# A hybrid RWKV-7 and latent-attention layer on one core: latents split once into fp32r pairs, all heads' values computed ahead of the sweeps, two slabs parked in HBM

## Chip, core and metric

The program runs on one core of a Trainium2 chip, in one launch. The metric is the device time of that core in microseconds; lower is better. TensorE does the matmuls (PE in the rows, PEld for its weight loads), VectorE is DVE, ScalarE is ACT, GpSimd is POOL, and the loads are issued from SyncE (SP).

## What is computed

One decoder layer over 1024 tokens of width 1024, in float32. The part that matters here is the latent attention (MLA):

```python
h = x @ w_in                                   # 2464 columns: r, k, v, ..., c_q (384), c_kv (256), k_pe (32)
q  = (rms_norm(c_q)  @ w_uq ).reshape(S, 8, 64 + 32)     # 32 rotary columns per head
kv = (rms_norm(c_kv) @ w_ukv).reshape(S, 8, 64 + 64)     # k_nope, v
s  = where(causal, q @ k.T * scale, -inf)
y_mla = softmax(s) @ v                         # per head, 128-query blocks
```

An RWKV-7 group uses the columns r, k, v of the same `h`; then follow the output projection, two LayerNorms and a feed-forward with 4096 hidden columns.

## The kernel before, in words

`hT` holds the transposed projection as 20 slabs of 128 columns by 1024 tokens: r is slabs 0 to 3, k 4 to 7, v 8 to 11, the latents c_q 14 to 16 and c_kv 17 and 18, the rotary key 19.
`project_in` computes `hT` slab by slab, latents first; ACT scales a slab out of PSUM (L283), DVE blends in the token shift (`mix`, L333). The latents are normalised in place (L397). The last pair of slabs is 12 and 13.

`mla` is a software pipeline over 8 heads. PE's order is written out in `sweep`: for each block of 128 keys, `st` (scores by three products, L593), ACT's exponential (L680), `pv` (probabilities by values, float32, L608), and in between, by the table `TURNS`, the pieces of the next head, which share PSUM banks 0 and 1:

```python
TURNS = {0: ("q", None), 1: ("k", None), 2: ("v", 7), 3: (6, 5), 4: (4, 3), 5: (2, 1), 6: (0, "m")}
```

`q_item` (L521) is 6 float32 matmuls of 512 columns, `k_item` (L531) 4 with 64 output rows, `v_item` (L541) 16 with 64 columns; the numbers are score blocks whose row maxima DVE takes (L747), and "m" transposes the maxima. `take` waits on `a_free`: bank 0 or 1 is handed back by the engine that read it. DVE's order per head is: remainder of q (L722), the two rotary products (L734, L735, from a copy `q_pe` that ACT made, L663), first part of the reciprocal for the head before (L761), remainder of k (L722), second part of that reciprocal, the quotient (L767), then all the maxima. Heads 0 and 1 come without the reciprocal parts. Ahead of the heads DVE clears a tile, rounds the rotary key for both buffers and the mask constants (L708 to L717). The eight heads run in loops of two. SP loads a head's weights two heads ahead (L497) and clears two HBM scratch areas at the start (L505).

`rwkv_inputs` follows; its SP part begins at L933, its first masked product goes out at L944, and `rwkv_chunks` reads slabs r, k and v of `hT`.

Of the kernel before, what the change touches and what calls it, by code (L numbers as in the profile page):

```python
# [153 lines left out]
def project_in(nc, mem, k, x, w_in, positions):  # L154
# [12 lines left out]
    sums = ps[:, 4, 0:RT * TT * 2].rearrange("p (c t h) -> p c t h", c=RT, t=TT)  # L167
    first = T_CQ // 2
# [16 lines left out]
    with ExitStack() as ctx:  # L185
# [12 lines left out]
            nc, ctx, "a_keys_squared", "a_keys_summed", "a_keys_rooted", "a_rotated", "a_ones_in")  # L198
        block = ctx.enter_context(nc.Block())
# [3 lines left out]
        def _(sp):  # L203
# [18 lines left out]
            with sp.Fori(0, first) as i:  # L222
                load(i, i + early)

# [47 lines left out]
        def _(act):  # L272
# [44 lines left out]
            nc.scalar.activation(k.key_norm[:], sums, ACT.Sqrt).then_inc(keys_rooted, 1)  # L317
            pair(6, 6 + early)

        @block.vector  # L320
        def _(dve):
# [72 lines left out]
            def normalise(n):  # L394
                tile0, tiles, gain, _ = LATENTS[n]
                for c in range(tiles):
                    nc.vector.scalar_tensor_tensor(hT[:, tile0 + c, :], hT[:, tile0 + c, :],  # L397
                                                   cols[:, gain + c:gain + c + 1], root[n][:], ALU.mult, ALU.mult)
# [23 lines left out]
            step.mark(nc.vector.reciprocal(k.key_norm[:], k.key_norm[:]))  # L422
            for j in range(2):
                mix(j, first - 1, trips - 1)

def mla(nc, mem, k, t):
# [3 lines left out]
    trig = mem.at("trig", 118, [P, S])  # L431
    q_hi = [mem.at(f"q_hi{p}", 126 + 4 * p, [P, S], F32R) for p in range(2)]
    q_lo = [mem.at(f"q_lo{p}", 134 + 4 * p, [P, S], F32R) for p in range(2)]
    k_hi = [mem.at(f"k_hi{p}", 142 + 4 * p, [P, S], F32R) for p in range(2)]
    k_lo = [mem.at(f"k_lo{p}", 150 + 4 * p, [P, S], F32R) for p in range(2)]
    v_one = [mem.at(f"v_one{p}", 158 + 4 * p, [P, TT, P]) for p in range(2)]
    probs = [mem.at(f"probs{n}", 166 + 4 * n, [P, S]) for n in range(3)]
    w_uq = [mem.at(f"w_uq{p}", 178 + 1.5 * p, [P, QLT, P]) for p in range(2)]
    w_ukv = [mem.at(f"w_ukv{p}", 181 + p, [P, KVLT, P]) for p in range(2)]
    rot_a = mem.at("rot_a", 183, [P, S])  # L440
    rot_b = mem.at("rot_b", 187, [P, S])
    recip, y_full = k.att_recip, k.att_y
    att = k.att
    q_pe = mem.at("q_pe", 203, [P, S])
# [21 lines left out]
    TAKES = [("q", (0, 1)), ("k", (0, 1)), ("v", (0,))]  # L466
# [11 lines left out]
    with ExitStack() as ctx:  # L478
        in_sem, trig_ready, key_ready, causal_rr, ones_set = sems(
            nc, ctx, "b_in", "b_trig_ready", "b_key_ready", "b_causal_r", "b_ones_set")  # L480
        q_pe_done, zeroed, zeros_out = sems(nc, ctx, "b_q_pe_done", "b_zeroed", "b_zeros_out")
        w_in = sems(nc, ctx, "b_w_in0", "b_w_in1")
        q_hi_done, k_hi_done, rot_ready, q_ready, m_ready = sems(
# [11 lines left out]
        @block.sync  # L495
        def _(sp):

            def load(h, p):
                sp.dma_start(w_uq[p][:], t["w_uq"][h]).then_inc(w_in[p], 16)
                sp.dma_start(w_ukv[p][:], t["w_ukv"][h]).then_inc(w_in[p], 16)  # L500
# [7 lines left out]
            with sp.Fori(1, NH // 2) as i:  # L508
                for p in range(2):
                    sp.wait_ge(item[0], USES[0] * (2 * i + p - 2) + nth("v", 0) + 1)  # L510
                    load(2 * i + p, p)

        @block.tensor
        def _(pe):
# [6 lines left out]
            def q_item(h, p, i, first):  # L521
                pe.wait_ge(w_in[p], 32 * (i + 1))
                for b in range(2):
                    if not first:
                        take(h, "q", b)
                    for c in range(QLT):
                        last = nc.tensor.matmul(ps[:, b, :], w_uq[p][:, c, :],
                                                hT[:, T_CQ + c, b * HALF:(b + 1) * HALF],
                                                start=c == 0, stop=c == QLT - 1)
                    last.then_inc(item[b], 1)  # L530

            def k_item(h, p):
                pe.wait_ge(q_pe_done, h + 1)
                for b in range(2):
                    take(h, "k", b)
                    for c in range(KVLT):
                        last = nc.tensor.matmul(ps[lo64, b, :], w_ukv[p][:, c, 0:HD],
                                                hT[:, T_CKV + c, b * HALF:(b + 1) * HALF],
                                                start=c == 0, stop=c == KVLT - 1)
                    last.then_inc(item[b], 1)  # L540

            def v_item(h, p):
                take(h, "v", 0)
                for tt in range(TT):
                    for c in range(KVLT):
                        last = nc.tensor.matmul(ps[:, 0, tt * HD:(tt + 1) * HD],
                                                hT[:, T_CKV + c, tt * P:(tt + 1) * P], w_ukv[p][:, c, HD:2 * HD],
                                                start=c == 0, stop=c == KVLT - 1)
                last.then_inc(item[0], 1)
# [48 lines left out]

            def pv(h, p, kt):
# [4 lines left out]
                for b in range(2):  # L604
# [3 lines left out]
                    last = nc.tensor.matmul(ps[:, O[b], lo - b * HALF:HALF], v_one[p][:, kt, :],  # L608
# [4 lines left out]
            def sweep(h, p, i, more):  # L613

                def turn(what):
# [3 lines left out]
                    if what == "q":  # L619
                        q_item(nh, np_, i + p, False)  # L620
                    elif what == "k":
                        k_item(nh, np_)
                    elif what == "v":
                        v_item(nh, np_)
# [13 lines left out]
            q_item(0, 0, 0, True)  # L638
            k_item(0, 0)
            v_item(0, 0)  # L640
# [6 lines left out]
            with pe.Fori(0, NH // 2 - 1) as i:  # L647
                for p in range(2):
                    sweep(2 * i + p, p, i, True)
            sweep(NH - 2, 0, NH // 2 - 1, True)  # L650
            sweep(NH - 1, 1, NH // 2 - 1, False)

        @block.scalar
        def _(act):
            def front(h, p, n):

                if n == 0:
# [3 lines left out]
                    if not (type(h) is int and h == 0):  # L661
                        act.wait_ge(q_ready, h)
                    nc.scalar.activation(q_pe[hi64, :], flat(A, hi64), ACT.Copy).then_inc(q_pe_done, 1)  # L663
                if n == 1:
                    for b in range(2):
                        act.wait_ge(item[b], USES[b] * h + nth("k", b) + 1)
                    nc.scalar.activation(k_hi[p][lo64, :], flat(A, lo64), ACT.Copy).then_inc(k_hi_done, 1)
                if n == 2:
                    act.wait_ge(item[0], USES[0] * h + nth("v", 0) + 1)
                    nc.scalar.activation(v_one[p][:, :, 0:HD], ps[:, 0, :].rearrange("p (t d) -> p t d", d=HD),  # L670
                                         ACT.Copy).then_inc(a_free[0], 1)
# [4 lines left out]
            def sweep(h, p, more):  # L676
                for kt in range(TT):
# [8 lines left out]
                    if more and kt == 2:  # L686
                        front(h + 1, 1 - p, 2)
# [7 lines left out]
            for n in range(4):  # L695
                front(0, 0, n)
            with act.Fori(0, NH // 2 - 1) as i:
                for p in range(2):
                    sweep(2 * i + p, p, True)
            sweep(NH - 2, 0, True)  # L700
            sweep(NH - 1, 1, False)

        @block.vector
        def _(dve):
            step = k.dve_steps.on(dve)
            V = nc.vector

            V.memset(zeros, 0.0).then_inc(zeroed, 1)  # L708
# [10 lines left out]
            def low_part(lo, hi):  # L719
# [1370 lines left out]
```

## Time and profile before

| | us |
|---|---|
| median of the runs (1686.79 to 1690.92) | 1690.69 |
| the profiled execution's own time | 1691.39 |
| its span, first to last instruction | 1689.6 |
| projection (start to the last slab's blend) | 0 to 265.5 |
| attention (`mla`) | 265.7 to 554.3 |
| feed-forward and last norm | from about 760 |

The span is 1.8 us less than the execution's time. Over the whole span PE is busy 92 percent, DVE 53, ACT 18, POOL 12, and TensorE's mean granted clock is 0.956 of full speed. A busy share says which engine has the most to do, not which wait ends last; for that the timeline of one head is read. A timeline row is start, duration, engine, line, operation and how many were merged; a bracket gives the idle time before it and what ended that.

### The profile page before, as it was taken

To read this page: it belongs to the slowest core of one execution; us is meant where nothing else is said; L and a number is where in the kernel's file an instruction comes from. 1 tells how busy PE (TensorE), PEld (TensorE's weight loads), DVE (VectorE), ACT (ScalarE), POOL (GpSimd) and SP (SyncE) were. 2 spreads that over 40 slices of the span, in tenths; PEclk is the share of its full clock that TensorE was granted. 3 is DMA by queue.
4 is the path that set the end of the run, shared out by engine and by line. 5 is a ranking of instruction groups with operands and counts; after the bars stand their busy time and mean duration, and the time that the engine had idled before them with its cause. 6 is when DMAs were issued, how large, how long until landed. Compare 5 with 4: busy or idle time off the path is not lost. (4 is left out here: it accounts for less than half of the span.)

```text
span 1689.6 us, 26357 instructions
## 1 busy us (share of the span) xinstructions
PE 1546.1 (92%) x11192; PEld 1239.7 (73%) x11192; DVE 888.6 (53%) x1077; ACT 307.7 (18%) x431; POOL 209.0 (12%) x134
## 2 busy tenths in 40 slices
PE   6999997999999718999789799999999999999994
PEld 5887884656666418998578688888888888888873
DVE  3254444356656863334747645555555555555559
ACT  2112201233333602322200210000000000000001
POOL 0000003124323350000106100000000000000005
PEclk8999988899999869999989899999999999999997
DMA  4111103000000162121050111111111111111002
GB/s 166 50 50 42 45 13 126 9 8 8 16 0 1 31 87 60 42 49 53 12 199 0 61 65 50 50 50 50 50 50 50 50 50 50 50 50 50 25 1 99
DMA packets 80507, 82.91 MB, mean 49 GB/s; under 512 B 63136, under 2 KB 65696, under 8 KB 78384
## 3 DMA queue, kind: packets, MB, share of 16 engines
q1 hardware_dynamic: 72176, 81.28, 14.6%
q10 hardware_dynamic: 8256, 0.52, 0.5%
q8 instruction: 61, 1.00, 0.2%
q14 instruction: 14, 0.11, 0.0%
HBM read 70.18 MB, written 11.60 MB: 48 GB/s over the span
## 5 line engine op out<-in xcount | busy, mean ns | idle before, releaser
L1907 DVE TENSOR_TENSOR x<-banks,x 128x512 f32<-128x512 f32 x256 | 171.4, 688 | 99.1 <-PE banks L1835 99.0
L1835 PE MATMUL banks<-w_hi,hid_hi 128*128 128x512 f32 x480 | 187.4, 390 | 2.3 <-DVE x L1907 2.3
L1835 PE MATMUL banks<-w_hi,hid_lo 128*128 128x512 f32 x480 | 187.4, 391 | 0.0
L1835 PE MATMUL banks<-w_lo,hid_hi 128*128 128x512 f32 x480 | 187.4, 390 | 0.0
L122 PE MATMUL banks<-x1T_hi,w_hi 128*128 128x512 f32 x512 | 157.7, 389 | 2.3 <-DVEq L1928 2.3
L122 PE MATMUL banks<-x1T_lo,w_hi 128*128 128x512 f32 x512 | 157.6, 389 | 0.0
L122 PE MATMUL banks<-x1T_hi,w_lo 128*128 128x512 f32 x512 | 157.6, 389 | 0.0
L1892 DVE TENSOR_TENSOR squared<-relu 128x1024 f32<-128x1024 f32 x32 | 39.2, 1226 | 224.9 <-ACT relu L1856 224.9
L1856 ACT ACTIVATE relu<-banks 128x1024 f32<-128x1024 f32 x32 | 32.9, 1029 | 589.0 <-PE banks L122 589.0
L122 PEld LDWEIGHTS banks<-x1T_hi,w_hi 128*128 128x128 f32 x512 | 96.0, 188 | 22.4 <-DVEq L1928 2.5
L122 PEld LDWEIGHTS banks<-x1T_hi,w_lo 128*128 128x128 f32 x512 | 96.1, 188 | 20.0
L122 PEld LDWEIGHTS banks<-x1T_lo,w_hi 128*128 128x128 f32 x512 | 96.1, 188 | 20.0
L1835 PEld LDWEIGHTS banks<-w_hi,hid_hi 128*128 128x128 f32 x480 | 90.5, 189 | 21.5 <-DVE x L1907 2.7
L122 PE MATMUL banks<-xT_hi,win_hi 128*128 128x512 f32 x320 | 101.0, 397 | 4.8 <-DVE xT_lo L404 4.8
L1835 PEld LDWEIGHTS banks<-w_hi,hid_lo 128*128 128x128 f32 x480 | 90.5, 188 | 18.8
L1835 PEld LDWEIGHTS banks<-w_lo,hid_hi 128*128 128x128 f32 x480 | 90.4, 188 | 18.8
L1974 POOL TENSOR_TENSOR x<-x,ln_gain 128x1024 f32<-128x1024 f32 x5 | 11.8, 2370 | 718.2 <-ACT x L1868 718.2
L122 PE MATMUL banks<-xT_lo,win_hi 128*128 128x512 f32 x320 | 100.2, 395 | 0.0
L122 PE MATMUL banks<-xT_hi,win_lo 128*128 128x512 f32 x320 | 99.7, 393 | 0.0
L333 DVE SCALAR_TENSOR_TENSOR hT<-banks,cols,hT 128x1023 f32 (+1 forms) x20 | 25.7, 1283 | 138.4 <-ACT hT L283 138.3
L608 PE MATMUL banks<-probs,v_one 128*128 128x512 f32 (+3 forms) x192 | 75.5, 507 | 0.0
L131 DVE TENSOR_TENSOR w_lo<-w_raw,w_hi 128x1024 fp32r<-128x1024 f32 (+1 forms) x47 | 73.6, 1566 | 1.6
(270 smaller groups left out, 2773.4 us busy)
## 6 DMA issues: line engine op xcount, KB each, us to landing
w_raw<-in_w_ffn SPq DMA_DIRECT2D x32, 512.0 KB, 5.9
w_raw<-in_w_ffn SPq DMA_DIRECT2D x16, 1024.0 KB, 4.8
win_raw<-in_w_in SPq DMA_DIRECT2D x20, 512.0 KB, 3.5
x_tok<-in_x SPq DMA_DIRECT2D x8, 512.0 KB, 7.6
wout_raw<-in_w_out SPq DMA_DIRECT2D x8, 512.0 KB, 4.7
x<-in_x SPq DMA_DIRECT2D x1, 4096.0 KB, 18.1
layer_out<-x SPq DMA_DIRECT2D x8, 512.0 KB, 2.6
inv_d<-ym_lo SPq DMA_DIRECT2D x4, 512.0 KB
```

The lines of the kernel that those rows point to most:

```text
L122: last = nc.tensor.matmul(out, w[:, kt, :], r(kt, b), start=kt == 0 and n == 0, stop=kt == tiles - 1 and n == 2)
L131: nc.vector.tensor_tensor(lo, raw, hi.bitcast(F32), ALU.subtract).then_inc(lo_sem, 1)
L333: nc.vector.scalar_tensor_tensor(hT[:, 2 * i + j, 1:S], flat[:, 0:S - 1], cols[:, bass.ds(C_MU + 2 * i + j, 1)], hT[:, 2 * i + j, 1:S], AL ...
L608: last = nc.tensor.matmul(ps[:, O[b], lo - b * HALF:HALF], v_one[p][:, kt, :], probs[kt % 3][:, lo:(b + 1) * HALF], start=kt == 0, stop=kt ...
L1835: last = nc.tensor.matmul(ps[:, 4 + n % 4, :], a[q][:, j, tok], w[:, j, col], start=j == 0 and m == 0, stop=j == GRP - 1 and m == 2)
L1856: A(relu[j][:], flat(2 * j), ACT.Relu).then_inc(relu_done, 1)
L1892: V.tensor_tensor(squared[j][:], relu[j][:], relu[j][:], ALU.mult).then_inc(relu_free, 1)
L1907: return V.tensor_tensor(piece, ps[:, 4 + n % 4, :], piece, ALU.add).then_inc(added, 1)
L1974: step.mark(G.tensor_tensor(acc[:, tt, :], acc[:, tt, :], gain[:], ALU.mult))
```

## The change

Five things. (1) After normalisation each of the five latent slabs is split once into `lat_hi` (ACT) and `lat_lo` (DVE). The room comes from slabs r, which SP stores to HBM (`r_d`) before; v is stored too (`v_d`), since attention's tiles now lie there. `rwkv_inputs` loads both back ahead of its other constants. (2) `q_item` becomes 18 fp32r matmuls, for which DVE splits each head's `w_uq`. (3) All heads' values are computed once, after head 0's keys, by 48 fp32r matmuls of 512 columns (`value_items`); `v_item` is gone. (4) `k_item` stays float32, but its two 512-token halves go to output rows 0 to 63 and 64 to 127. (5) ACT's copy `q_pe` is gone: DVE takes the rotary products straight from PSUM, and now before the remainder of q. The loops over heads are written out.

```diff
@@ project_in
+            for j in range(2):
+                sp.wait_ge(h_mixed[j], early + 2)
+            sp.dma_start(k.r_d, hT[:, T_R:T_R + RT, :]).then_inc(r_out, 16)
...
+            sp.dma_start(k.v_d, hT[:, T_V:T_V + RT, :]).then_inc(v_out, 16)
+            sp.wait_ge(v_out, 16)
...
+            act.wait_ge(r_out, 16)
+            for c in range(QLT + KVLT):
+                act.wait_ge(normed, c + 1)
+                nc.scalar.activation(k.lat_hi[c][:], hT[:, T_CQ + c, :], ACT.Copy).then_inc(latents_hi, 1)
             pair(6, 6 + early)
...
+            for c in range(QLT + KVLT):
+                dve.wait_ge(latents_hi, c + 1)
+                nc.vector.tensor_tensor(k.lat_lo[c][:], hT[:, T_CQ + c, :], k.lat_hi[c][:].bitcast(F32), ALU.subtract)
             for j in range(2):
                 mix(j, first - 1, trips - 1)
@@ mla
-    TURNS = {0: ("q", None), 1: ("k", None), 2: ("v", 7), 3: (6, 5), 4: (4, 3), 5: (2, 1), 6: (0, "m")}
+    TURNS = {0: ("q", None), 1: ("k", None), 2: (None, 7), 3: (6, 5), 4: (4, 3), 5: (2, 1), 6: (0, "m")}
...
-            load(0, 0)
+            load(0)
+            for h in range(NH):
+                sp.dma_start(wv_raw[:, :, h, :], t["w_ukv"][h][:, :, HD:2 * HD]).then_inc(wv_in, 16)
             sp.dma_start(causal[:], t["causal"]).then_inc(in_sem, 16)
-            load(1, 1)
+            load(1)
...
+                pe.wait_ge(w_split[p], h // 2 + 1)
                 for b in range(2):
                     if not first:
                         take(h, "q", b)
+                for c in range(QLT):
+                    for n, (w, r) in enumerate(((wq_hi, lat_hi), (wq_hi, lat_lo), (wq_lo, lat_hi))):
+                        for b in range(2):
+                            last = nc.tensor.matmul(ps[:, b, :], w[p][:, c, :], r[c][:, b * HALF:(b + 1) * HALF],
+                                                    start=c == 0 and n == 0, stop=c == QLT - 1 and n == 2)
...
             def k_item(h, p):
-                pe.wait_ge(q_pe_done, h + 1)
                 for b in range(2):
                     take(h, "k", b)
+                for c in range(KVLT):
+                    for b in range(2):
+                        last = nc.tensor.matmul(ps[64 * b:64 * b + 64, b, :], w_uk[p][:, c, :],
                                                 hT[:, T_CKV + c, b * HALF:(b + 1) * HALF],
...
-            q_item(0, 0, 0, True)
+            q_item(0, 0, True)
             k_item(0, 0)
-            v_item(0, 0)
+            value_items()
...
         @block.vector
+            split_w(0)
+            dve.wait_ge(wv_in, 16 * NH)
+            split2(nc, dve, wv_raw[:], wv_hi[:], wv_lo[:], wv_rounded, 1, wv_split)
+            split_w(1)
             V.memset(zeros, 0.0).then_inc(zeroed, 1)
...
             def front_q(h, p, first=False):
-                dve.wait_ge(q_hi_done, h + 1)
-                low_part(q_lo[p], q_hi[p])
-                dve.wait_ge(q_pe_done, h + 1)
+                for b in range(2):
+                    dve.wait_ge(item[b], USES[b] * h + nth("q", b) + 1)
...
+                V.tensor_tensor(rot_a[pe32, :], flat(A, pe32), trig[pe32, :], ALU.mult).then_inc(rot_ready, 1)
+                V.tensor_tensor(rot_b[pe32, :], flat(A, sw32), trig[sw32, :], ALU.mult).then_inc(rot_ready, 1)
+                dve.wait_ge(q_hi_done, h + 1)
+                low_part(q_lo[p], q_hi[p], False)
...
+            for h in range(2, NH):
+                front_q(h, h % 2)
+                invert(h - 2, 0)
+                front_k(h, h % 2)
+                invert(h - 2, 1)
+                leave(h - 2, h % 2)
+                maxima(h, h % 2)
+                if h + 2 < NH:
+                    split_w(h + 2)
@@ rwkv_inputs
             sp.dma_start(w_lora[:], t["w_lora"]).then_inc(loaded, 16)
+            sp.dma_start(hT[:, T_V:T_V + RT, :], k.v_d).then_inc(reloaded, 16)
+            sp.dma_start(hT[:, T_R:T_R + RT, :], k.r_d).then_inc(reloaded, 16)
             sp.dma_start(k.gate[:], t["gate_g2"]).then_inc(later_in, 16)
...
+            sp.wait_ge(reloaded, 32)
```

## Rows read from the trace of the kernel before

**Rows 1.** The page: busy time, share of the span and instructions of each engine

```profile
PE 1546.1 (92%) x11192; PEld 1239.7 (73%) x11192; DVE 888.6 (53%) x1077; ACT 307.7 (18%) x431; POOL 209.0 (12%) x134
```

**Rows 2.** Timeline, one steady head (front of head 5 within the sweep of head 4)

```profile
444.73 1.02 ACT L660 ACTIVATE q_hi<-banks 64x1024 fp32r<-64x1024 f32 x1 [3.77 <-PE banks L527]
...
445.78 1.28 DVE L722 TENSOR_TENSOR q_lo<-banks,q_hi 64x512 fp32r<-64x512 f32 x2 [8.81 <-ACT q_hi L660]
...
446.92 3.64 PE L537 MATMUL banks<-hT,w_ukv 128*64 128x512 f32 x8 [0.89 <-ACT q_pe L663]
447.10 1.22 DVE L734 TENSOR_TENSOR rot_a<-q_pe,trig 32x1024 f32<-32x1024 f32 x1
...
450.60 1.02 ACT L667 ACTIVATE k_hi<-banks 64x1024 fp32r<-64x1024 f32 x1 [2.87 <-PE banks L537]
...
452.96 4.95 DVE L761 RECIPROCAL att_recip<-att 64x768 f32<-64x768 f32 x1
...
453.50 3.68 PE L546 MATMUL banks<-w_ukv,hT 128*128 128x64 f32 x32
...
459.19 1.29 DVE L747 TENSOR_REDUCE row_max_parts<-banks 128x1 f32<-128x512 f32 x2
...
460.30 0.68 PE L561 MATMUL banks<-k_hi,q_hi 96*128 96x512 f32 x2
```

**Rows 3.** Timeline of PE, eleven fp32r matmuls of 512 columns apart: first and last

```profile
1499.62 0.39 PE L1835 MATMUL banks<-w_lo,hid_hi 128*128 128x512 f32 x1
...
1501.89 0.39 PE L1835 MATMUL banks<-w_hi,hid_lo 128*128 128x512 f32 x1
```

**Rows 4.** Timeline of PE in the RWKV chunks, products on both halves of the array

```profile
661.17 0.57 PE L1298 MATMUL banks<-inverse_t,product 64*64 64x64 f32 x14
```

**Rows 5.** Timeline, DVE's first maxima of head 1, which have no reciprocal before them

```profile
325.20 1.29 DVE L747 TENSOR_REDUCE row_max_parts<-banks 128x1 f32<-128x512 f32 x2 [6.06 <-PE banks L561]
```

**Rows 6.** Timeline, DVE's remainder of q for heads 3 and 4

```profile
378.98 1.28 DVE L722 TENSOR_TENSOR q_lo<-banks,q_hi 64x512 fp32r<-64x512 f32 x2 [8.83 <-ACT q_hi L660]
...
412.10 1.28 DVE L722 TENSOR_TENSOR q_lo<-banks,q_hi 64x512 fp32r<-64x512 f32 x2 [8.34 <-ACT q_hi L660]
```

**Rows 7.** Timeline of the start of attention

```profile
265.73 0.34 SPq L499 DMA_DIRECT2D w_uq<-in_w_uq  x1
...
266.97 2.91 DVE L710 CAST k_hi<-key_rot 32x1024 fp32r<-32x1024 f32 x2
...
272.66 0.07 DVE L770 MEMSET row_max_parts<- 128x16 f32 x1
...
278.30 3.65 PE L537 MATMUL banks<-hT,w_ukv 128*64 128x512 f32 x8 [2.22 <-ACT q_pe L663]
...
289.24 1.19 PE L561 MATMUL banks<-k_hi,q_hi 96*128 96x512 f32 x2 [0.78 <-ACT v_one L670]
```

**Rows 8.** DMA issues of the chunk stage, 256-byte pieces: size, median us to landing

```profile
inverse_t<-inv_t_d SPq DMA_DIRECT2D x18, 64.0 KB, 2.4
```

**Rows 9.** Timeline, SP's issues of such copies

```profile
635.80 1.26 SPq L1202 DMA_DIRECT2D inverse_t<-inv_t_d  x2
```

**Rows 10.** Groups by line and shape, DVE's remainder of a 128x1024 weight tile

```profile
L131 DVE TENSOR_TENSOR win_lo<-win_raw,win_hi 128x1024 fp32r<-128x1024 f32 x20 | 24.5, 1226 | 0.7
```

**Rows 11.** Timeline of PE in `rwkv_inputs`, after a wait

```profile
596.41 3.07 PE L979 MATMUL banks<-kk,beta 64*64 64x64 f32 x64 [2.62 <-DVE kk L1065]
```

**Rows 12.** Windows: length, busy time of PE, PEld, DVE, ACT, POOL, granted clock, DMA

```profile
597.00:598.00 1.00, 1.00 (x30) 1.00 (x27) 1.00 (x2) 0.00 (x0) 1.00 (x1) 0.59 0.14 31
598.00:602.00 4.00, 3.79 (x92) 3.60 (x89) 2.77 (x2) 0.00 (x0) 0.58 (x1) 0.67 0.73 141
```

**Rows 13.** Timeline of the end of the projection: the last slab's blend

```profile
264.18 1.28 DVE L333 SCALAR_TENSOR_TENSOR hT<-banks,cols,hT 128x1023 f32<-128x1023 f32 x1 [9.59 <-ACT hT L283]
```

**Rows 14.** The page: a load of 4 MB, size and us to landing

```profile
x<-in_x SPq DMA_DIRECT2D x1, 4096.0 KB, 18.1
```

**Rows 15.** Timeline of SP in `rwkv_inputs`: the first store that waits for the constants

```profile
592.82 5.99 SPq L944 DMA_DIRECT2D low_d<-low_keys  x4
```

More of the change, by code:

```diff
@@ L221, in _ @@
                 load(i, i - first)
-            with sp.Fori(0, first) as i:
+            with sp.Fori(0, 4) as i:
                 load(i, i + early)
+            for j in range(2):
+                sp.wait_ge(h_mixed[j], early + 2)
+            sp.dma_start(k.r_d, hT[:, T_R:T_R + RT, :]).then_inc(r_out, 16)
+            with sp.Fori(4, first) as i:
+                load(i, i + early)
+            for j in range(2):
+                sp.wait_ge(h_mixed[j], early + 6)
+            sp.dma_start(k.v_d, hT[:, T_V:T_V + RT, :]).then_inc(v_out, 16)
+            sp.wait_ge(v_out, 16)
         @block.tensor
@@ L507, in _ @@
                 sp.dma_start(part, zeros[0:part.shape[0], :]).then_inc(zeros_out, 16)
[L508 to L511, printed above, removed]
+            for h in range(2, NH):
+                sp.wait_ge(w_split[h % 2], h // 2)
+                for b in range(2):
+                    sp.wait_ge(item[b], USES[b] * (h - 2) + nth("k", b) + 1)
+                load(h)
         @block.tensor
@@ L525, in q_item @@
                         take(h, "q", b)
[L526 to L530, printed above, removed]
+                for c in range(QLT):
[3 more added lines that the diff above has]
+                                                    start=c == 0 and n == 0, stop=c == QLT - 1 and n == 2)
+                            if c == QLT - 1 and n == 2:
+                                last.then_inc(item[b], 1)
@@ L545, in v_item @@
                     for c in range(KVLT):
[L546 to L549, printed above, removed]
+                        for n, (r, w) in enumerate(((lat_hi, wv_hi), (lat_lo, wv_hi), (lat_hi, wv_lo))):
+                            last = nc.tensor.matmul(ps[:, 2 + tt % 6, :], r[QLT + c][:, at],
+                                                    w[:, c, :, :].rearrange("p h d -> p (h d)"),
+                                                    start=c == 0 and n == 0, stop=c == KVLT - 1 and n == 2)
@@ L597, in st, with values_and_ones @@
                 last.then_inc(st_ready, 1)
+            def values_and_ones(h, kt):
+                pair = v_all[:, kt, h // 2, :, :].rearrange("p a d -> p (a d)")
+                return pair[:, 64 * (h % 2):64 * (h % 2) + P]
             def pv(h, p, kt):
@@ L611, in pv, with sweep @@
                 last.then_inc(pv_done, 1)
-            def sweep(h, p, i, more):
+            def sweep(h, p, more):
                 def turn(what):
@@ L646, in _ @@
             pe.wait_ge(ones_set, 1)
[L647 to L651, printed above, removed]
+            pe.wait_ge(v_out, TT)
+            for h in range(NH):
+                sweep(h, h % 2, h < NH - 1)
         @block.scalar
@@ L666, in front @@
                         act.wait_ge(item[b], USES[b] * h + nth("k", b) + 1)
[L667 to L671, printed above, removed]
+                    for b in range(2):
+                        nc.scalar.activation(k_hi[p][lo64, b * HALF:(b + 1) * HALF], ps[64 * b:64 * b + 64, b, :],
+                                             ACT.Copy).then_inc(k_hi_done, 1)
                 if n == 3:
@@ L694, in _ @@
             act.sem_inc(exp_done, T_FREE)
[L695 to L701, printed above, removed]
+            front(0, 0, 0)
+            front(0, 0, 1)
+            for tt in range(TT):
+                act.wait_ge(v_mm, tt + 1)
+                nc.scalar.activation(v_all[:, tt, :, 0:3:2, :],
+                                     ps[:, 2 + tt % 6, :].rearrange("p (i a d) -> p i a d", a=2, d=HD), ACT.Copy)\
+                    .then_inc(v_out, 1)
+            front(0, 0, 3)
+            for h in range(NH):
+                sweep(h, h % 2, h < NH - 1)
         @block.vector
@@ L823, in _ @@
             step.wait()
-            for p in range(2):
-                last = G.memset(v_one[p][:, :, HD:P], 1.0)
-            last.then_inc(ones_set, 1)
+            G.memset(v_all[:, :, :, 1, :].rearrange("p t i d -> p (t i) d"), 1.0).then_inc(ones_set, 1)
             pool.wait_ge(ones_set, 1)
```

125 lines of the change are left out of this document (66 added, 59 removed).

## The prediction

> **What bounds the kernel now.** I read the page first: PE is busy 92 percent [rows 1], and the change takes PE work away, which looks like a gain of the same size. A busy share is no critical path, so the timeline of one steady head comes next [rows 2]. There two things run side by side between the end of the q item (call it Q, 444.73, where ACT begins to read it) and the first maxima. PE runs scores, keys, values and `pv` with one gap of 0.89 us. DVE runs a fixed chain: remainder of q (1.28), two rotary products (1.22 each), reciprocal parts, remainder of k, 4.95 of reciprocal, quotient, and the first maximum begins at 459.19, Q+14.5. PE's next score block (qt 6) needs the bank that this maximum frees; it starts at 460.30, Q+15.6. Both arrive together: PE has no slack there and DVE has none either. The values item, which ends just before, is what keeps PE occupied while DVE inverts.
>
> **The change, part by part.** All sums stand against the profiled execution, 1691.4 us, which is 0.7 above the median of the runs (1690.7).
>
> *Queries.* Before, 12 instructions of 512 columns. Their pace is that of the keys, 8 in 3.64 with a tail of some 0.2 [rows 2], 0.427 us each: 5.1 us. After, 18 fp32r instructions at (1501.89 − 1499.62) / 10 = 0.227 us [rows 3]: 4.1 us. Gain 1.0 us per head, seven heads beside a sweep; it lies ahead of Q, on the path.
>
> *Values.* Before, 3.68 less the tail of some 0.2, 3.5 us per head, up to 457.0 [rows 2]. Gone.
>
> *Keys.* Before 8 × 0.427 = 3.4 us. The new order is half 0 (two passes), half 1 (two passes), twice over. Fourteen passes of 64 columns on distinct rows and columns of the array took 0.57 us [rows 4], where in turn, at 0.427 × 64 / 512 = 0.053 each, they would need 0.75: neighbours on separate array parts overlap. If halves that share all rows do so too, a pass of one half lies beside a pass of the other, and 8 passes take 5 slots, 2.1 us. Bounds: 1.7 (all in pairs) and 3.4 (none). I take 2.1.
> The Trainium skill (TensorEngine Tiling, Key Properties) says that tiles operate independently, and its list of configurations has 128×64 as two tiles; by that the item would take 1.7 to 2.1, and by a plain reading of in-order issue 3.4. No row of before has two halves over the same rows.
>
> *The chain after Q.* This part decides. DVE now does the rotary products first: 2.5 us, then the remainder of q, 1.3, and only that frees the banks. Keys start at Q+3.9; PE has finished its scores at 446.92 − 0.89, Q+1.3, so its gap grows from 0.9 to 2.6 us. Keys end at Q+6.2 (Q+5.8 before). ACT copies the halves in two pieces, between 0.5 (half of its 1.02) and 1.0 each; I take 0.6. Then remainder of k 1.3, reciprocal 4.95, quotient with its hand-over 1.25 (459.19 − 457.91): the first maximum begins at Q+15.1, against Q+14.5. PE: keys issued by Q+6.0, `pv` and scores 3.2 (450.33 to 453.50), no values, then 3.3 (457.02 to 460.30) brings it to block 6 at Q+12.5. The block waits for the first maximum, until Q+15.8, and its second half for the second, so what follows is 0.5 us later after Q than before. So the 3.5 us of values and 1.3 of keys turn into an idle of 3.3 us, and a steady head gains 1.0 − 0.5 = 0.5 us. Six heads (2 to 7): −3 us.
>
> *Head 1* has no reciprocal before its maxima; there DVE sat idle 6.06 us for PE [rows 5]. It gains in full: 1.0 + 3.5 + 1.3, less 1.7 of the longer gap: −4 us.
>
> *Written-out loops.* Remainder of q comes 33.1 us after its predecessor where a loop body runs on (378.98 to 412.10 [rows 6]) and 33.7 where the loop turns (to 445.78 [rows 2]). Three turns: between 0 and −2; I take −2. Fetching the longer program is between 0 and a few us; straight code elsewhere keeps PE busy, so 0.
>
> *Head 0.* PE cannot start the keys until the remainder of q has freed the banks, and DVE's queue has new work in front of it. SP starts at 265.7 [rows 7]; ten issues stand up to the last values load, nine of them 256-byte pieces at 0.63 [rows 9], and such a copy lands in 2.4 [rows 8]: about 274.2. Splitting the values' weights costs 1.2 [rows 10] plus a cast of less than that, a head's weights 0.8 more: 277. Then the old chain of clearing and casting, 266.0 to 272.7 [rows 7], so it ends near 283.7. Products and remainder: 287.5. Keys start there, not at 278.3 [rows 7], at half clock after so long a wait (5 × 0.85 = 4.3): 291.8. Then 48 fp32r matmuls, 10.9 us and about 1 for the clock's return: 303.8. The first score block follows; it was at 289.24 [rows 7]. +14 us, between +10 (loads land early, keys in pairs) and +17 (loads at half that pace). On the queue behind SP's new loads stand the mask, head 1's weights and the HBM clears; the mask is needed at 283, the clears at the end.
>
> *Clock.* A wait of 2.22 us at the start of attention left the keys at full pace (3.65 for 8 [rows 7], as in the steady head). A wait of 2.62 us [rows 11] was followed by a fall from 2.4 to 1.2 GHz 1.2 us later (granted clock 0.59 in that us [rows 12]). The new idle of 3.3 us before block 6 is past both, so I count one fall per head, 2 to 7. That fall was over after 3.4 us (0.59 of full speed in one us and 0.67 in the next four are 0.8 and 2.6 us at half [rows 12]). It costs half its length where PE is the busy one, which it is after block 6: 1.7 each, 6 of them, +10. The other gap, 2.6 us, lies at the edge; I count it at nothing and keep it as a rival.
> The Trainium skill (TensorE: Matmul & The Clock Gate, "A second HAM failure mode") says that TensorE's small idles between groups of matmuls can swing the clock; no number of mine is taken from it.
>
> *Projection.* ACT's 5 copies and DVE's 5 remainders (1.2 each) fall before the last slab, while PE works: DVE waited 9.59 us for the last blend [rows 13]. If they were late, the blend would be, by at most 5 × 1.2. The stores, 2 MB each, are half of a load of 18.1 us [rows 14], and v goes out with a whole slab pair of PE work to come. Zero.
>
> *Reload.* 4 MB ahead of the constants, 18 us on the queue [rows 14], so they land near 577 plus what attention loses; the first product that needs them goes out at 592.8 [rows 15]. Zero, and if that cover failed a few us.
>
> Sum: 1691.4 + 14 − 4 − 3 − 2 + 10 = 1706.4; against the median 1706.
>
> **Rivals.**
> *The clock holds.* The short idles let it stay up: 1696. For it: the 2.22 us wait. Against it: that waits of 2.62 us already told.
> *The wait before the keys.* Rotary products ahead of the remainder make 2.6 us of idle, equal to the one that told. If the clock falls there too, the keys run at half pace on DVE's chain: 1.9 us in each of 7 heads, +13: 1719. From 2.2 to 2.6 us it decides.
> *The halves do not overlap.* The change then does not do what it says: 1.3 us more per head on the chain, for 7 heads and head 0, +10: 1716.
> *PE work counts in full (faster).* If DVE's chain reached its maxima before PE does, at Q+12.5 or earlier, 2.6 us sooner than I add up, then all removed work would tell: queries 8, values 3.5 × 8 − 11 = 17, keys 10, loops 2, less head 0's late start of about 14 and the added gaps, which overlap in part: 1670. For it: PE's 92 percent. Against it: every term of that chain is a measured row, and the reciprocal stays.
>
> **How the numbers follow.** Forecast (1701 to 1711) 0.40. Clock holds 0.20; half of that falls within 0.3 percent, which is 5 us and about what a measurement of this kernel can tell from no change. Wait before the keys 0.13, no overlap 0.10, PE in full 0.17. So faster 0.17, same 0.10, slower 0.73. The range 1688 to 1720 leaves out most of the last case and the worst of the slower ones, some 2 in 10.
>
> **What would show it.** Right: first scores of head 1 some 14 us later; DVE's values split ahead of its clearing; PE waiting about 2.6 us before keys and 3.3 us before block 6 for a maximum; half clock after it; keys in 2.1 to 2.4 us; head 1's maxima no longer waiting for PE. Wrong: a head period well below 32 us, maxima that wait for PE, or the keys of head 0 starting before 285.

## The result, and the profile after

| | before | after |
|---|---|---|
| median of the runs, us | 1689.59 (1686.79 to 1690.92, 4 runs) | 1706.38 (1700.32 to 1709.89, 4 runs) |
| ratio, 95 percent interval | | 1.0098 (1.0063 to 1.0133) |
| the profiled execution's own time, and its span | 1691.39, 1689.6 | 1704.15, 1702.3 |
| mean granted clock | 0.956 | 0.943 |
| start of attention (first weight load) to the first score block of head 0 | 23.5 | 35.3 |
| attention, start to the load of `w_lora` | 289.1 | 306.4 |
| from there to the end | 1134.8 | 1131.2 |

The changed kernel was run a second time in a later batch: 1704.38, ratio 1.0097 (1.007 to 1.0124), as expected (1700 to 1710). It is slower: 16.8 us by the medians of each of the two batches (1706.38 against 1689.59, 1704.38 against 1687.61), 12.7 us between the two profiled executions. (Time and profile before gave 1690.69 as the median; that is the higher of the two middle values.) Medians here leave out four executions in a much slower state: two of the kernel before, 2022 and 2024 us, and two of experiment 2, 3151 and 3982 us.

All of the loss arises in attention. The other stages scatter by a few us from one execution to the next: the last row of the table was 1131.2 in this execution, 1134.5 in the second one, and 1134 to 1138 in all other kernels of this study, and attention began anywhere between 261.1 and 266.6 us. From here on the length of attention in the profiled execution is therefore read beside the time.

The page first: busy time by engine. Before it was 1546.1 for PE [rows 1].

```profile
PE 1521.8 (89%) x11032; PEld 1230.5 (72%) x11032; DVE 903.9 (53%) x1100; ACT 303.3 (18%) x434; POOL 208.6 (12%) x133
```

PE has 24 us less work, and the span is 12.7 us longer: the time in which PE does nothing grew by 37 us. Where it grew, the timeline of one steady head of the changed kernel says (front of head 6, within the sweep of head 5). It answers to [rows 2]; Q is 491.31, where DVE begins the rotary products.

```profile
491.31 1.22 DVE L782 TENSOR_TENSOR rot_a<-banks,trig 32x1024 f32<-32x1024 f32 x1 [5.29 <-PE banks L563]
...
493.83 1.28 DVE L771 TENSOR_TENSOR q_lo<-banks,q_hi 64x512 fp32r<-64x512 f32 x2
...
495.14 1.75 DVE L812 RECIPROCAL att_recip<-att 64x256 f32<-64x256 f32 x1
...
495.26 1.94 PE L574 MATMUL banks<-hT,w_uk 128*64 128x512 f32 x8 [2.71 <-DVE q_lo L771]
...
497.30 1.21 ACT L708 ACTIVATE k_hi<-banks 64x512 fp32r<-64x512 f32 x2 [3.79 <-PE banks L574]
...
498.54 1.41 DVE L771 TENSOR_TENSOR k_lo<-banks,k_hi 64x512 fp32r<-64x512 f32 x2 [1.65 <-ACT k_hi L708]
...
499.98 4.95 DVE L812 RECIPROCAL att_recip<-att 64x768 f32<-64x768 f32 x1
...
506.21 2.73 DVE L797 TENSOR_REDUCE row_max_parts<-banks 128x1 f32<-128x512 f32 x4
...
506.96 1.29 PE L603 MATMUL banks<-k_hi,q_hi 96*128 96x512 f32 x2 [3.44 <-DVE row_max_parts L797]
```

The keys wait 2.71 us for the remainder of q. The product of block 6 waits 3.44 us for the first maximum, which stands behind 4.95 of reciprocal on DVE. DVE in turn waits 5.29 us for the q item: within one head each engine waits for the other in turn. The wait before the keys comes back in heads 1 to 7, the one before block 6 in heads 2 to 7 (waits of the changed kernel from 300 to 554 us; a row is who waited for whom, total us, times, longest; the 11 of the first row include short ones):

```profile
PE banks L603 <- DVE row_max_parts L797: 21.2, 11, 3.5
PE banks L574 <- DVE q_lo L771: 18.9, 7, 2.7
```

What the clock does behind the wait before block 6 stands in the windows (length, busy time of PE, PEld, DVE, ACT, POOL, granted clock, DMA share, GB/s); the last row is another head's keys, those at 425.46, after the same wait of 2.70 us:

```profile
506.00:507.00 1.00, 0.04 (x1) 0.05 (x1) 0.97 (x3) 0.00 (x0) 0.74 (x1) 1.00 0.00 0
507.00:508.00 1.00, 0.97 (x2) 0.59 (x3) 0.93 (x2) 0.00 (x0) 1.00 (x1) 0.62 0.00 0
508.00:510.00 2.00, 2.00 (x6) 1.30 (x6) 0.81 (x2) 0.00 (x0) 1.92 (x2) 0.50 0.00 0
510.00:511.00 1.00, 1.00 (x4) 0.51 (x3) 0.00 (x0) 0.00 (x0) 0.56 (x1) 0.67 0.00 0
511.00:515.00 4.00, 4.00 (x23) 3.19 (x22) 2.60 (x5) 0.80 (x2) 0.00 (x0) 1.00 0.00 0
...
427.00:429.00 2.00, 2.00 (x7) 0.33 (x3) 0.10 (x1) 0.00 (x0) 1.92 (x2) 0.57 0.00 0
```

Half clock follows the wait before block 6 in each of the six heads that have it, for some 3.4 us in five of them and 6.8 us in head 3. The keys ran at full clock in heads 5 to 7 (1.94 us for 8), as in the head shown; in heads 1 to 4 they ran mostly at half (3.2 to 3.7 us; 3.54 at 425.46). The starts of the rotary products are 35.4, 36.9 and 35.7 us apart from head 2 to head 5, and 34.1 and 34.1 from there; before, a head took 33.1 to 34.0. Before, the granted clock was 1.00 over all of 310 to 554 us.

Head 0, on the timeline, answers to [rows 7]:

```profile
276.24 0.91 DVE L756 MEMSET ym_lo<- 128x1024 f32 x1 [0.16 <-issue]
...
281.63 1.22 DVE L782 TENSOR_TENSOR rot_a<-banks,trig 32x1024 f32<-32x1024 f32 x1 [0.36 <-DVE row_max_parts L822]
...
285.57 3.52 PE L574 MATMUL banks<-hT,w_uk 128*64 128x512 f32 x8 [9.06 <-DVE q_lo L771]
...
289.02 0.50 PE L588 MATMUL banks<-wv_hi,latent_hi 128*128 128x512 f32 x1
...
300.03 0.63 PE L603 MATMUL banks<-k_hi,q_hi 96*128 96x512 f32 x2
```

DVE's old clearing chain starts only at 276.24, behind the split of the values' weights; PE waits 9.06 us for it, and the first score block stands at 300.03.

### The profile page after: what moved, and what is told of

Its sections match the earlier page's. It is cut to its first block and busy times, and to the rows that moved or that the text cites. A ratio compares the mean times of both kernels' runs of the same rounds, so it can differ in the third digit from the quotient of the medians.

```text
span 1702.3 us, 25673 instructions
## 1 busy us (share of the span) xinstructions
PE 1521.8 (89%) x11032; PEld 1230.5 (72%) x11032; DVE 903.9 (53%) x1100; ACT 303.3 (18%) x434; POOL 208.6 (12%) x133
## 3 DMA queue, kind: packets, MB, share of 16 engines
q1 hardware_dynamic: 75952, 89.67, 15.8%
## 5 line engine op out<-in xcount | busy, mean ns | idle before, releaser
L2025 POOL TENSOR_TENSOR x<-x,ln_gain 128x1024 f32<-128x1024 f32 x5 | 11.8, 2369 | 716.9 <-ACT x L1919 716.9
L655 PE MATMUL banks<-probs,v_all 128*128 128x512 f32 (+3 forms) x192 | 84.1, 556 | 0.0
```

Source lines behind the costliest of these rows:

```text
L655: last = nc.tensor.matmul(ps[:, O[b], lo - b * HALF:HALF], values_and_ones(h, kt), probs[kt % 3][:, lo:(b + 1) * HALF], start=kt == 0, sto ...
L2025: step.mark(G.tensor_tensor(acc[:, tt, :], acc[:, tt, :], gain[:], ALU.mult))
```

## The experiments

All compare with the changed kernel's 1704.4 to 1706.4 us and its 306 us of attention.

**1. Half of the reciprocal ahead of the query item.** DVE sits idle 5.29 us before the rotary products; this puts work there.

```diff
-                cut = (slice(0, S // 4), slice(S // 4, S))[n]
+                cut = (slice(0, S // 2), slice(S // 2, 3 * S // 4), slice(3 * S // 4, S))[n]
...
             for h in range(2, NH):
-                front_q(h, h % 2)
                 invert(h - 2, 0)
-                front_k(h, h % 2)
+                front_q(h, h % 2)
                 invert(h - 2, 1)
+                front_k(h, h % 2)
+                invert(h - 2, 2)
                 leave(h - 2, h % 2)
```

> Edit to the changed kernel: the reciprocal for the head before is cut in three and its first half (512 columns, about 3.3 us) is done before the rotary products, where DVE sits idle 5.3 us; the rest stays in its two old places. Chain theory (DVE's fixed chain after Q sets when block 6 may start, and the idle there drops the clock): the wait before block 6 shrinks from 3.4 us to at most 0.5, the fall of the clock after it goes, a steady head takes about 29.5 us instead of 34.1, six heads give 28 us: about 1678 us where the changed kernel has 1706. Rival (the heads are bound by what PE and the clock do, and the place of the reciprocal is indifferent): within 3 us of 1706.

Measured: 1681.02, ratio to before 0.9958 (0.9938 to 0.9979), attention 278.2. The same waits:

```profile
PE banks L574 <- DVE q_lo L771: 18.9, 7, 2.7
...
PE banks L603 <- DVE row_max_parts L797: 2.5, 7, 0.5
```

Of the two waits only the one before block 6 went, from 3.5 to at most 0.5 us, and heads take 29.4 to 30.6 us. That one wait with the half clock behind it is 23 to 25 us of time. The removed PE work was real; it stood behind DVE's queue. The wait before the keys is as long as ever, and in six of the seven heads the keys behind it ran partly at half clock (2.7 to 3.6 us, 1.94 in the seventh). So this clock loss is still in the 1681; experiments 3 and 9 take it away.

**2. The same in the kernel before**, where by [rows 2] DVE and PE reach the maxima together.

> Edit to the kernel before: the same move of the reciprocal's first half ahead of the front of q. Theory (before the change PE's values item filled the time of DVE's chain, so both arrived together and PE had no gap): at most 1 us per head, 1684 to 1690 us. Rival (DVE's chain bound the kernel before, too): 3 us per head, about 1672 us.

Measured: 1688.91 against 1689.55 of the kernel before in the same batch, ratio 0.999 (0.9976 to 1.0004). The reorder is worth nothing that can be told from no change where PE has the values to compute meanwhile (heads 2 to 7 are 33.0 to 33.5 us apart, before 33.1 to 34.0). So the gain of experiment 1 is the change's own, held back by DVE, and not one that either kernel could have had.

**3. The idle filled.** Matmuls whose results nobody reads, in both gaps (9 before the keys of heads 1 to 7, 13 before block 6 of heads 2 to 7): the waits shrink to 0.65 and 0.5 us, DVE's chain stays.

```diff
                     if what == "k":
+                        fill(h, 0, 9)
+                    if what == 6 and nh >= 2:
+                        fill(h, 2, 13)
```

> Edit to the changed kernel: in the two gaps of a head PE runs idle-time matmuls of 512 fp32r columns into a score bank that is free (9 before the keys, 13 before block 6), so PE is busy but nothing is done sooner; the output is untouched. Clock theory (each wait costs its own length and, on top, half speed for 3.4 us after it): granted clock 2.4 GHz throughout the sweeps, block 6 no earlier after Q, but a head about 1.7 us shorter, six heads, and as much again for three of the waits before the keys: 1691 to 1696 us. Rival (the falls cost nothing since DVE is late anyway): 1706.

Measured: 1689.9, ratio 1.0003 (0.9983 to 1.0022), attention 289.8. Windows, in which only PE's work and the clock matter:

```profile
314.00:430.00 116.00, 110.92 (x509) 77.82 (x507) 73.33 (x92) 32.30 (x46) 40.84 (x18) 1.00 0.04 10
430.00:540.00 110.00, 105.31 (x496) 74.87 (x495) 70.90 (x85) 32.03 (x47) 33.83 (x15) 1.00 0.01 3
```

In the changed kernel the same view has 0.87 for 314 to 430 and 0.94 for 430 to 554. More work for PE, and 15 to 16 us less time. Block 6 still starts at Q+15.6 (457.42 against 441.78 in head 5), so the gaps are as long as before, and what has changed is the clock behind them: this is the half clock's price alone. Heads 2 to 7 take 32.6 us each. It is not the whole loss of the change, since the gaps themselves stay behind the filling; experiment 1 removes one of them and gets 9 us more.

**4. Both key halves on output rows 0 to 63**, one after the other, so that they cannot lie beside each other.

```diff
-                for c in range(KVLT):
-                    for b in range(2):
-                        last = nc.tensor.matmul(ps[64 * b:64 * b + 64, b, :], w_uk[p][:, c, :],
+                for b in range(2):
+                    for c in range(KVLT):
+                        last = nc.tensor.matmul(ps[lo64, b, :], w_uk[p][:, c, :],
```

> Edit to the changed kernel: both 512-token halves of the keys go to output rows 0 to 63, one half after the other, as before the change. Theory (the pairing halves the item, and the item lies on DVE's chain): the keys take 3.6 us instead of 1.9 and the first maximum comes 1.5 us later in each head, seven heads and head 0: about 1718 us. Rival (the keys hide beside something): 1706.

Measured: 1725.19, ratio 1.0222 (1.0194 to 1.0249), attention 325.5, a steady head 37.5 us. Timeline:

```profile
466.34 5.03 PE L574 MATMUL banks<-hT,w_uk 128*64 128x512 f32 x8 [2.71 <-DVE q_lo L771]
...
480.86 1.29 PE L603 MATMUL banks<-k_hi,q_hi 96*128 96x512 f32 x2 [3.18 <-DVE row_max_parts L797]
```

and the window behind that block:

```profile
480.00:486.00 6.00, 5.14 (x11) 3.43 (x12) 3.14 (x7) 0.00 (x0) 4.23 (x2) 0.50 0.00 0
```

Worse than expected by 7 us. The halves side by side save not 1.3 us per head but 1.7 at full clock and more behind a wait: here the item ran partly at half clock in every head (5.0 to 5.3 where full clock gave 3.64 in [rows 2]). The half clock behind block 6 also lasts 6.8 us in each of the six heads, twice as long as in most heads of the changed kernel. The pairing, with what it spares in clock, is worth 19 to 21 us to the changed kernel.

**5. Head 0's queries ahead of its values** on DVE.

```diff
-            split_w(0)
-            dve.wait_ge(wv_in, 16 * NH)
-            split2(nc, dve, wv_raw[:], wv_hi[:], wv_lo[:], wv_rounded, 1, wv_split)
-            split_w(1)
             V.memset(zeros, 0.0).then_inc(zeroed, 1)
+            split_w(0)
...
+            dve.wait_ge(wv_in, 16 * NH)
+            split2(nc, dve, wv_raw[:], wv_hi[:], wv_lo[:], wv_rounded, 1, wv_split)
```

> Edit to the changed kernel, DVE's order at the start of attention alone: clearing and rotary-key rounding first, then head 0's query weights, then the values' weights; the weights of head 1 are split after the remainder of head 0's keys. Theory (the keys of head 0 waited for DVE's queue, 9.1 us of PE idle): keys of head 0 start at about 280.5 instead of 285.6, the first score block at about 293.5 instead of 300.0, the sweeps are unchanged: 6.5 us less than the changed kernel, about 1700. Rival (the start is bound by the loads or by the clock): within 2 us of 1706.

Measured: 1701.03, ratio 1.0069 (1.0042 to 1.0096); the first score block at +30.9 after the start of attention against +35.3, so 4.4 us earlier, of the 6.5 expected. Of the 2.1 that are missing, 0.7 lie before the keys, since PE begins its q item 1.1 us later and ends it 0.6 later. The other 1.4 lie behind them: keys and values take 14.5 us as in the changed kernel, partly at half clock, where the expectation left 13.0. Attention is 299.7 us, 6.7 less than the changed kernel's; the further 2.3 us arise in the sweeps, where the keys ran slow in three heads, not four. The keys of head 0 (timeline):

```profile
282.64 2.82 PE L574 MATMUL banks<-hT,w_uk 128*64 128x512 f32 x8 [4.04 <-DVE q_lo L770]
```

**6. The copy of the rotary parts put back** (heads 1 to 7): ACT copies them, DVE takes the remainder of q first, banks come free earlier.

```diff
+                        nc.scalar.activation(q_pe[hi64, :], flat(A, hi64), ACT.Copy).then_inc(q_pe_done, 1)
...
+                if h:
+                    dve.wait_ge(q_hi_done, h + 1)
+                    low_part(q_lo[p], q_hi[p], False)
+                    dve.wait_ge(q_pe_done, h)
...
+                    V.tensor_tensor(rot_a[pe32, :], q_pe[pe32, :], trig[pe32, :], ALU.mult).then_inc(rot_ready, 1)
+                    V.tensor_tensor(rot_b[pe32, :], q_pe[sw32, :], trig[sw32, :], ALU.mult).then_inc(rot_ready, 1)
```

> Edit to the changed kernel: ACT's copy of the rotary half of q is back for heads 1 to 7 (in the room of a latent tile that only the values read), and DVE takes the remainder of q first and the rotary products after it, from the copy. Theory: keys start about Q+2.2 instead of Q+3.95, PE's wait before them is 0.9 instead of 2.7 us and no fall of the clock follows it; but the products then stand between the remainder of q and the remainder of k, so the first maximum comes only about 0.6 us earlier, and the wait before block 6 stays at 3.5 to 4 us. 0.6 in seven heads and 2 us in each of the three heads that fell there: 1696 to 1700 us. Rival (the keys' early start carries through to the end of the head): 1.7 us per head, 1694 or less with no fall: about 1690.

Measured: 1703.33, ratio 1.0084 (1.0057 to 1.0112), level with the changed kernel's 1704.38 of the same batch: a miss by the time. Attention is 299.6 us against 306.0, a gain of the size expected, but it began 4.8 us later (266.6 against 261.8) than in the changed kernel's execution of that batch; with a scatter of that size outside attention, four executions can't tell the two apart. The mechanism was missed in any case. The keys waited 1.25 us in place of 2.7 and ran in 1.94 in all seven heads; and then (waits, and a window behind block 7 of head 5, which starts at 464.68):

```profile
PE banks L606 <- POOL q_lo L869: 21.2, 7, 3.0
```

```profile
466.00:472.00 6.00, 5.77 (x13) 3.34 (x13) 3.36 (x5) 0.70 (x1) 4.23 (x2) 0.50 0.00 0
```

Block 7 needs GpSimd's rotated queries, which come 7.1 us after the second product (three operations of 2.34). Put behind the remainder and a copy, they end last. Half clock follows that wait of 3.0 us in six of the seven heads, each time for 6.8 us. So the change's order, products first, pays 1.5 us before the keys to be on time there: GpSimd's last operation ends at 500.97 and block 7 starts at 501.22 in the changed kernel.

**7. Experiments 1, 5 and 6 together.**

> The changed kernel with the early reciprocal, the order of head 0 and the rotary copy together. Theory: the reciprocal no longer hides behind the keys, so the keys' earlier start now carries through: a steady head takes about 28 us (29.4 with the early reciprocal alone), the start is 6.5 us shorter: about 1664 us, under both kernels. Rival (the parts share one gain): about 1675.

Measured: 1694.45, ratio 1.0032 (1.0014 to 1.0051), attention 292.0. A miss by 20 to 30 us: the wait for GpSimd is 3.0 us in each of 7 heads again, with half clock behind it in six. The rotary copy alone is what parts this version from experiment 8, and it costs 19 us there.

**8. Experiments 1 and 5 alone.**

> The changed kernel with the two edits that helped alone: half of the earlier head's reciprocal ahead of the query item, and head 0's queries ahead of its values. Theory (the two act in different places, one in heads 2 to 7 and one in head 0, so they add): 1681 less the 4 us that head 0's order gave by itself, about 1677, with the wait of the block-6 product at 0.5 us and block 7 of head 0 at +31. Rival: the half clock of head 0 takes it back, 1681.

Measured: 1675.1 (1669.9 to 1679.31), ratio 0.9925 (0.9898 to 0.9953), attention 274.3, the wait before block 6 at most 0.3 us. They add: 4 us of attention less than experiment 1, and 1677 was expected.

**9. Keys one turn later,** behind the first product with the earlier head's values, and the reciprocal in two halves, both ahead of the key remainder. The cut is against experiment 8; the third call of `invert` goes too.

```diff
-    TURNS = {0: ("q", None), 1: ("k", None), 2: (None, 7), 3: (6, 5), 4: (4, 3), 5: (2, 1), 6: (0, "m")}
+    TURNS = {0: ("q", None), 1: (None, "k"), 2: (None, 7), 3: (6, 5), 4: (4, 3), 5: (2, 1), 6: (0, "m")}
...
-                cut = (slice(0, S // 2), slice(S // 2, 3 * S // 4), slice(3 * S // 4, S))[n]
+                cut = (slice(0, S // 2), slice(S // 2, S))[n]
```

> As the kernel with both edits, with the rest of the reciprocal between the query item and the key halves; the key turn stands one place later in TensorE's order, behind the first product with the values of the earlier head (1.7 us). Theory (what costs is a TensorE wait of over 2 us with half clock behind it): the product fills most of the 2.7 us wait ahead of the keys, which falls to about 1.0, the heads take 28.5 to 29.5 us, and the time is 1665 to 1671. Rival (the keys come later by what the product takes, and so do key halves, maxima and block 6): the wait ahead of block 6 comes back at 2 us or more, 1677 to 1685. A third: GpSimd's rotation of the queries ends last, as in the kernel that copied the rotary parts back, and TensorE waits for it ahead of block 7, 1680 to 1695.

Measured: 1665.31 (1659.42 to 1667.74), ratio 0.9854 (0.9832 to 0.9876), attention 262.6, a steady head 28.5 us. Its waits, and then a head on its timeline:

```profile
PE banks L574 <- DVE q_lo L770: 6.9, 7, 1.0
PE banks L603 <- POOL q_lo L856: 6.8, 7, 1.0
```

```profile
429.70 1.88 PE L655 MATMUL banks<-probs,v_all 128*128 128x512 f32 x4
432.57 1.94 PE L574 MATMUL banks<-hT,w_uk 128*64 128x512 f32 x8 [0.99 <-DVE q_lo L770]
...
438.32 0.74 PE L603 MATMUL banks<-k_hi,q_hi 96*128 96x512 f32 x2 [0.95 <-POOL q_lo L856]
```

Both waits are 1.0 us, the keys took 1.94 us in all seven heads, the granted clock was 1.00 from 314 to 430, and GpSimd is the next in line. One head took 30.1 us: between 466 and 476 the clock fell once all the same, although no wait there was longer than 1.0 us. The two edits, PE's turn and the place of the reciprocal, were not run apart. This version beats the kernel before by 1.5 percent and the changed one by 40 us.

**10. The query item in float32 again,** 12 instructions on the upper part of the latents with the raw weights; the remainders of latents and weights in the query are left out.

```diff
-                    for n, (w, r) in enumerate(((wq_hi, lat_hi), (wq_hi, lat_lo), (wq_lo, lat_hi))):
+                    for b in range(2):
+                        last = nc.tensor.matmul(ps[:, b, :], w_uq[p][:, c, :],
+                                                lat_hi[c][:, b * HALF:(b + 1) * HALF].bitcast(F32),
```

> The changed kernel with the query projection as float32 on the latents' upper part alone, 12 instructions, in place of 18 fp32r ones (the raw weights, no remainders of weight or latents in the query: that part of the computation is left out). By the measured pace of float32 keys, 0.427 us each, the item takes 5.1 us in place of 18 by 0.227, 4.1 us. Theory (the query item lies on the path that starts each head in the changed kernel, since block 6 waits for a chain that begins at its end): 1.0 us for each of 8 heads, 8 us above the changed kernel, about 1713. Rival (VectorE's chain from the earlier head ends last, so the item's own length is hidden): within 3 us of the changed kernel.

Measured: 1711.59, ratio 1.0134 (1.0115 to 1.0154), 5 to 7 us above the changed kernel, attention 313.3, 7 us longer. On the timeline the item takes

```profile
491.16 5.31 PE L562 MATMUL banks<-latent_hi,w_uq 128*128 128x512 f32 x12
```

So three fp32r products in place of float32 are worth the 1 us per head that the sum gave them, and this saving reaches the end: it lies ahead of Q.

## Why the prediction was right

The stretches of the profiled executions, forecast and measured, against before:

| stretch | forecast | measured |
|---|---|---|
| projection, up to the first weight load | 0 | −1.0 |
| from there to the first score block of head 0 | +14 | +11.8 |
| from there to the end of the q item of head 2 (head 1) | −4 | −5.6 |
| heads 2 to 7, loops, clock (−3 − 2 + 10) | +5 | +11.1 |
| after attention | 0 | −3.6 |
| sum | +15 | +12.7 |

*The chain after Q* was the step that decided, and it held: first maximum at Q+14.9 (forecast 15.1, though its own terms add up to 14.9), block 6 at Q+15.65 (15.8), its wait 3.44 (3.3), the wait before the keys 2.7 (2.6). What it makes of a head without the clock shows in experiment 3: 32.6 us, where the loop bodies that ran on took 33.1, which is the 0.5 us of gain forecast. The rival in which PE's work counts in full needed a shorter chain; experiment 1 shows that it is DVE's order which kept it from coming true: 1681, and with head 0's order, PE's turn and the reciprocal moved too (experiment 9), 1665.

*Values.* Their 3.5 us per head turned into idle, as forecast, and experiment 2 shows it from the other side: with the values still in the sweep an early reciprocal is worth nothing that the runs can tell.

*Queries.* 1.0 us per head: the item took 4.1 us (486.96 to 491.06), and experiment 10 confirms that the difference reaches the end.

*Keys.* I took 2.1 us between 1.7 and 3.4. All in pairs was right: 1.94 with its tail, and 3.5 at half clock at the start. The Trainium skill (TensorEngine Tiling, Key Properties) says that tiles operate independently; the trace agrees, with 8 passes of 512 columns in 1.94 us against 3.64 [rows 2], although neighbours in the order go to the same half. The rival in which they do not overlap was priced at 1716; experiment 4 gives 1725, because I had left out that a longer item meets the half clock.

*Head 0.* +11.8 for +14. The splits ended at 276.1, 0.9 us earlier than worked out (the loads had landed by 272.8, not 274.2), and the old chain behind them took 5.0 us where it took 6.7 before: rounding the rotary key twice took 1.29 us, against 2.91 before and in experiment 5, where GpSimd's clearing ran beside it (that this is the reason was not tested). So the keys started at 285.6 for 287.5. At half clock they took 3.5, not 4.3, by the pairs; and the 48 value matmuls ran at full clock from the first (289.02 to 300.03, 0.229 each), so no time for the clock's return was due. The order on DVE was the cause; turning it gives 4.4 back (experiment 5), while computing the values costs its 11 us either way.

*Head 1.* −5.6 for −4, and for −5 if the query item of head 2, which lies in this stretch, is counted here. It did not come as worked out. Up to the end of head 1's q item the gain is 2.7 us where the query item gives 1.0: before the change this stretch ran at half clock from 289 to 307, now from 306 to 316 only. Behind it the gain is 2.9 us in place of 4.1, since the keys took 3.61 us at half clock. One of the signs fails too: head 1's maxima still wait for PE, 2.09 us for the first of them (6.06 in [rows 5]), and its first scores come 7 us later after the start of attention, not 14.

*Clock.* One fall per head behind block 6: as forecast, and 3.4 us long in five heads of six; its price is 1.5 us (34.1 against 32.6 in experiment 3) for 1.7. The rival in which the clock holds was priced at 1696; experiment 3 is that case and gives 1690, in part since heads 0 and 1 came cheaper than forecast. The step that failed is the gap that "lies at the edge": 2.7 us before the keys, counted at nothing. Behind it the keys of heads 1 to 4 ran slow and those of 5 to 7 did not. Heads 2 to 4 are 1.3, 2.8 and 1.6 us longer than 34.1, together 5.7 us, nearly the excess of that line of the table; in head 3 the fall behind block 6 was longer too (granted clock 0.50 over all of 402 to 408). Without it heads 2 to 7 come to +5.4 for +5. The rival that had it fall in each head (1719) is thus true for four of seven; in experiment 4 it is true for all. What decides between two heads with the same wait of 2.70 us no run tells; it stays open. The length of the wait alone does not: the wait of 2.22 us in head 0, from which the prediction took that the clock holds, was followed by half clock in experiment 2 (granted clock 0.57 from 279 to 283):

```profile
277.70 5.34 PE L537 MATMUL banks<-hT,w_ukv 128*64 128x512 f32 x8 [2.22 <-ACT q_pe L663]
```

*After attention,* −3.6: not a gain. The second execution of the same kernel has 1134.5 there, within 0.4 of before.

*Reload and projection.* Zero each, and zero within the scatter (−1.0 here, −4.0 in the second execution): v landed 8.5 and r 13.0 us after their issue at 571.5 and 571.9, before the inputs' products; DVE waited 8.59 us for the last blend (9.59 in [rows 13]).

So the mechanism was right, and the total, 1706 for a median of 1706.38, partly by luck: terms of head 0 and head 1 too unfavourable by 2 each, a clock term too small by 6, and 5 us of scatter in stages outside.

## What to carry to other kernels

Work taken from the busiest engine is worth what the next engine's queue lets through: lay the two engines' chains of one iteration side by side, and see what the second one must have done when the first one arrives. If it comes late, move its oldest ready work (here a reciprocal) into its own idle time before judging the change; with that and two further moves the same kernel went from 1 percent slower to 1.5 percent faster. Waits on TensorE such as these, of 2.3 to 3.5 us, are best split or filled with useful work of another stage, since here they cost about half as much again in clock (1.5 us behind one of 3.44). And behind the second engine's order stands a third engine (here GpSimd's 7 us chain), so count that one before moving its producer. Last, where the stages that a change leaves alone scatter by 5 us, read the stage that it touches beside the total.

## What the runs showed of the hardware that was not expected

- Two float32 matmuls with 64 output columns each, on the two halves of the array and over the same 128 rows, run beside each other with different moving data: 8 passes of 512 columns in 1.94 us, 3.64 before; at half clock 3.52.
- The same wait of 2.7 us before the keys was followed by partly half clock in some heads and not in others: 4 of 7 in the changed kernel (the same four in its second execution) and in experiment 10, 3 of 7 in experiment 5, 6 of 7 in experiments 1 and 8, 7 of 7 in experiment 4. Behind waits of 0.65 to 1.25 us (experiments 3, 6, 7, 9) the keys ran in 1.94 us in all 28 cases.
- The wait before block 6, of 2.3 to 3.5 us, was followed by half clock in all 30 cases (six heads each in the two executions of the changed kernel and in experiments 4, 5 and 10). The wait of 3.0 us before block 7 was followed by it in 12 of 14 (experiments 6 and 7). It lasted 3.4 us in some cases and 6.8 in others.
- Once, in experiment 9, the clock fell although no wait near it was longer than 1.0 us.
- Adding 22 matmuls per head with no use (9 in head 1) made the kernel 15 us faster (experiment 3).
